# DeltaNet gate joined to the output projection, and layer-end steps shared out anew, in a two-layer hybrid backbone

## The chip, the core and the metric

The kernel runs on one core of a Trainium2 chip. The metric is the device time of one execution in microseconds (us). TensorE is PE, VectorE is DVE, ScalarE is ACT, GpSimd is POOL and SyncE is SP in the rows of the profile.

## The reference

Two post-norm layers act on 1024 latent tokens and 256 context tokens, with 1024 channels, all in float32. In each layer one input projection feeds four groups of heads (windowed attention, a gated DeltaNet, retention, latent attention), whose joined outputs go through one output projection, and then an MLP with squared ReLU follows. The parts that matter here are these:

```python
def layer_norm(x, g, b):
    mu = jnp.mean(xf, axis=-1, keepdims=True)
    var = jnp.mean(jnp.square(xf - mu), axis=-1, keepdims=True)
    return (xf - mu) * lax.rsqrt(var + LN_EPS) * g + b
...
    def out(o, z_):        # DeltaNet gate
        o = rms_norm(o.transpose(0, 2, 1, 3), norm_g) * silu(z_)
...
        y, yc = token_mixers(x * (1 + sc1) + sh1, xc * (1 + csc1) + csh1, ...)
        x = layer_norm(DEEPNORM_ALPHA * x + g1 * (y @ w_out[layer]), ln1_g[layer], ln1_b[layer])
        x = layer_norm(DEEPNORM_ALPHA * x + g2 * squared_relu_mlp(x * (1 + sc2) + sh2, ...),
                       ln2_g[layer], ln2_b[layer])
```

The context goes through the same steps in layer 0 only, and the output is the latent stream.

## The kernel before

**Layout.** Channels lie on the 128 partitions: `X[:, k, token]` holds block k of 8 channel blocks for 1280 tokens. Tokens are worked in segments, `SEGMENTS` = (0, 256), (256, 768), (768, 1280); the first is the context. Layer 1 needs no context output and uses the last two (`tokens(L)`), and its very end is cut as (256, 768), (768, 1024), (1024, 1280) (`end_tokens`).

**Products.** Each float32 operand of a large product is split into a high part (rounded to fp32r) and a low part (the rest), and a product is three matmuls per channel block: high by high, low by high, high by low. The high part of the projection's input is `H_hi`, a copy by ScalarE (L1773); the low part `Y_lo` is a subtraction on VectorE (L2459), written over `Y` itself. Weight halves come by DMA into a ring and are split in the same way, by ScalarE (`split_high`, L1466) and VectorE (`split_low`, L1986) outside the MLP, and by GpSimd (L2731, L2732) in it. `next_half` makes TensorE wait until a half is split (`w_split`).

**Order.** Every engine has an instruction list of its own, and semaphores tie them together. `nth` and `tally` keep the counts. `ln.barrier()` makes all four engines wait for one another, and `link` makes an engine wait for its own last result.

**The gate.** After the DeltaNet scan, and behind a barrier, `gate` runs on ScalarE and VectorE and `gate_turn` on TensorE, once in each layer. The scan's output `o` and the gate input `z` have tokens on the partitions, 10 tiles of 256 channels. ScalarE squares `o` (L1755), takes tanh(z/2) (L1756), splits the high part of a weight half, takes a root (L1760, with a table load ahead of it) and splits a second one. VectorE sums the squares per head (L2359), makes (tanh + 1) z (L2362), multiplies by the gain `dn_g` (L2364), splits a low part (L1986), inverts the root (L2368) and then, in five rounds of two tiles, scales and gates (L2372, L2374). Each round is transposed by TensorE (L762, four transposes) and copied from PSUM into `Y` by ScalarE (L1765). A second barrier follows, then `project_out`: high parts, low parts, and 24 matmuls (L751) for each of 8 output blocks and each segment. Sums for the next normalization are made on VectorE between them.

**The layer end.** After the last MLP group each segment goes through `layer_end`. Its column sum goes through a matmul with ones (`end_mean`, L1249), `centre` subtracts the mean (L2392, VectorE), `square` squares on ScalarE into `Hm` (L1787), `end_var` sums the squares with ones on TensorE (L1257), `root` (L1792) and `invert` (L2399) work in PSUM, `scale` multiplies (L2405), and `affine` applies gain and bias, eight ScalarE instructions per segment (L1874). At the end of layer 0 the next layer starts at once: `modulate_full` (L1995, VectorE) makes the modulated input, `modulate_high` (L1481, ScalarE) its high part, written over `X` once `X` has been saved to memory (`x_saved_*`, SP's queue), and `modulate_low` (L2005, VectorE) the low part. `mla_item` steps of the latent attention's preparation are woven in on all engines; their one-column steps on GpSimd are `mla_prep` (L2634). GpSimd has no other work at either layer end. At the end of layer 1 the output is sent by SP in six transfers, each behind an `ln_out` count.

GpSimd has a step of the same form as an affine step elsewhere, in the MLP's start: `TS(X, X, grown_g, grown_b)` at L2744.

## Time and profile before

| | |
|---|---|
| median of 3 runs | 4320.06 us (4316.73 to 4320.37) |
| profiled execution | 4329.14 us, its span 4327.3 us |
| mean granted TensorE clock | 0.955 |
| TensorE busy | 3989.3 us (92%) |
| VectorE busy | 2041.8 us (47%) |
| ScalarE busy | 1131.9 us (26%) |
| GpSimd busy | 937.3 us (22%) |

Busy time is a sum over the span; a span is the time from the first to the last instruction. In a timeline a row gives the start and the length in us, engine, line, operation, output and inputs, shapes, how many instructions were merged, and in brackets the idle time before it and what ended it. ACTq, DVEq and POOLq are the engines' sequencers. Layer 0 has its gate from 1209 us and its end from 2245 us; layer 1 has its gate from 3421 us and its end from 4270 us.

### The profile page before, as it was taken

The numbers are of one execution on the slowest core, as the hardware profiler recorded it, in microseconds if no ns is written. First come the engines' busy times: TensorE is split into PE (matmuls) and PEld (weight loads), VectorE is DVE, ScalarE is ACT, GpSimd is POOL, SyncE is SP. The second block draws the span as 40 slices with busy tenths as digits, with TensorE's granted clock in tenths as the row PEclk, the third lists the DMA queues.
The fourth block names the chain that finished last, engine by engine and source line by source line (L and its number), as shares of the span: only waits on it lengthen the run. The fifth ranks groups of instructions, "written<-read, shape, count | busy, mean of one in ns | idle before, by whom it ended". The sixth has DMA issues, their size and how long they took to land. (4 is left out here: it accounts for less than half of the span.)

```text
span 4327.3 us, 77639 instructions
## 1 busy us (share of the span) xinstructions
PE 3989.3 (92%) x33178; PEld 3278.3 (76%) x33178; DVE 2041.8 (47%) x3705; ACT 1131.9 (26%) x2456; POOL 937.3 (22%) x671
## 2 busy tenths in 40 slices
PE   6999988989979999999998999889899799999997
PEld 5655987778867888888886557778688677888886
DVE  3344546544456433333356344566344555443346
ACT  3344224233323111111115443232333311110012
POOL 0000110032202433333321000100223114444441
PEclk8898999999989999999998998999899899999999
DMA  4311000100010111111111110000100011111111
GB/s 168 117 79 59 21 30 1 76 3 3 3 49 10 39 39 39 39 39 39 39 38 69 59 79 30 20 21 20 48 3 3 21 39 39 49 48 48 48 49 49
DMA packets 27552, 181.00 MB, mean 42 GB/s; under 512 B 2560, under 2 KB 6912, under 8 KB 12032
## 3 DMA queue, kind: packets, MB, share of 16 engines
q1 hardware_dynamic: 25968, 173.69, 10.8%
q8 instruction: 226, 3.70, 0.4%
q10 hardware_dynamic: 1296, 3.10, 0.2%
q14 instruction: 62, 0.51, 0.0%
HBM read 168.39 MB, written 8.39 MB: 41 GB/s over the span
## 5 line engine op out<-in xcount | busy, mean ns | idle before, releaser
L1298 PE MATMUL ps<-Yn_parts,ring_parts 128*128 128x512 f32 (+1 forms) x3888 | 803.2, 368 | 11.5 <-issue 7.7
L1298 PEld LDWEIGHTS ps<-Yn_parts,ring_parts 128*128 128x128 f32 x3888 | 674.4, 190 | 137.3 <-issue 9.9
L1298 PE MATMUL ps<-temp_parts,ring_parts 128*128 128x512 f32 (+1 forms) x2560 | 727.9, 370 | 3.9 <-DVE Hn_parts L2437 3.9
L2731 POOL TENSOR_TENSOR ring_parts<-ring,consts 128x2048 fp32r<-128x2048 f32 x64 | 295.6, 4619 | 1209.1 <-DMA ring<-in_ff 1093.6
L741 PE MATMUL ps<-ring_parts,Xn_parts 128*128 128x256 f32 x2560 | 514.6, 296 | 28.3 <-DVE ring_parts L1986 12.8
L2384 DVE SCALAR_TENSOR_TENSOR Xn<-ps,mods,Xn 128x256 f32<-128x256 f32 (+1 forms) x364 | 251.8, 692 | 604.0 <-PE ps L1298 503.3
L1298 PEld LDWEIGHTS ps<-temp_parts,ring_parts 128*128 128x128 f32 x2560 | 466.4, 190 | 88.3 <-DVE Hn_parts L2437 5.9
L1298 PE MATMUL ps<-Hn_parts,ring_parts 128*128 128x512 f32 (+1 forms) x1280 | 472.1, 369 | 0.0
L741 PEld LDWEIGHTS ps<-ring_parts,Xn_parts 128*128 128x128 f32 x2560 | 425.8, 199 | 32.3 <-issue 23.5
L1825 ACT ACTIVATE Yn<-ps 128x256 f32<-128x256 f32 (+1 forms) x160 | 88.7, 554 | 1265.7 <-PE ps L1298 1265.7
L2491 DVE TENSOR_TENSOR Yn<-Yn 128x256 f32<-128x256 f32 (+1 forms) x160 | 200.6, 1254 | 406.2 <-ACT Yn_parts L1827 406.2
L741 PE MATMUL ps<-ring_parts,Hn_parts 128*128 128x256 f32 x1280 | 371.7, 290 | 0.0
L762 PE MATMUL ps<-consts,temp 128*128 128x128 f32 (+1 forms) x1416 | 259.3, 300 | 94.4 <-DVE temp L2087 23.6
L762 PEld LDWEIGHTS ps<-consts,temp 128*128 128x128 f32 (+1 forms) x1416 | 175.9, 149 | 212.0 <-issue 96.4
L2732 POOL TENSOR_TENSOR ring_parts<-ring,ring_parts 128x2048 fp32r<-128x2048 f32 x64 | 302.2, 4722 | 5.0
L1298 PEld LDWEIGHTS ps<-Hn_parts,ring_parts 128*128 128x128 f32 x1280 | 242.4, 189 | 40.5
L741 PEld LDWEIGHTS ps<-ring_parts,Hn_parts 128*128 128x128 f32 x1280 | 255.8, 200 | 1.2 <-issue 0.2
L862 PE MATMUL ps<-Yn,temp 96*128 96x512 f32 (+1 forms) x400 | 199.0, 612 | 8.0 <-ACT temp L1565 3.9
L2339 DVE TENSOR_TENSOR ring<-ps,Hn 128x256 f32<-128x256 f32 x200 | 84.7, 423 | 237.3 <-PE ps L1168 236.3
L2492 DVE TENSOR_TENSOR Yn_parts<-Yn,Yn_parts 128x256 fp32r<-128x256 f32 (+1 forms) x160 | 193.0, 1206 | 5.5
L1730 ACT ACTIVATE ring<-ps 128x256 f32<-128x256 f32 x240 | 91.6, 382 | 363.3 <-PE ps L1179 310.2
L1576 ACT ACTIVATE temp<-ps 128x512 f32<-128x512 f32 (+1 forms) x200 | 103.8, 520 | 231.1 <-PE ps L762 217.9
(310 smaller groups left out, 5956.0 us busy)
## 6 DMA issues: line engine op xcount, KB each, us to landing
ring<-in_ff SPq DMA_DIRECT2D x64, 1024.0 KB, 4.7
ring<-in_ada SPq DMA_DIRECT2D x22, 2048.0 KB, 8.9
ring<-in_halves SPq DMA_DIRECT2D x28, 1024.0 KB, 4.8
Xn<-in_x SPq DMA_DIRECT2D x2, 5120.0 KB, 25.0
Hn<-in_ada SPq DMA_DIRECT2D x2, 2048.0 KB, 20.9
kept_x<-Xn SPq DMA_DIRECT2D x4, 1024.0 KB, 4.0
Xn<-kept_x SPq DMA_DIRECT2D x1, 4096.0 KB, 14.9
Hn<-in_halves SPq DMA_DIRECT2D x2, 1024.0 KB, 7.6
```

The source lines that it names most:

```text
L741: m = pe.matmul(ps[:, bank, 0:256], (G_hi, H_lo)[a][:, k, t * P:(t + 1) * P], w[b][:, k, :], start=(k == 0 and part == 0), stop=(k == KT - ...
L762: return pe.transpose(out, src, ident[0:rows, 0:rows])
L862: m = pe.matmul(m_flat[:, base + a:base + b], m_q[0:96, h, t * P:(t + 1) * P], m_k[0:96, h, a:b], start=True, stop=True, skip_group_check= ...
L1298: m = pe.matmul(ps[:, bank, 0:hi - lo], w[a][:, k, j * P:(j + 1) * P], x[b][:, k, lo:hi], start=(k == 0 and part == 0), stop=(k == k_n - 1 ...
L1576: A(m_pT[:, k0:k1, :], ps[:, 5 + c % 2, 0:(k1 - k0) * P].rearrange("p (a b) -> p a b", b=P), ACT.Copy)\
L1730: A(flat(b["lower"]), ps[:, q, 0:256], ACT.Copy).then_inc(sems[f"u_lower{q}"], tally(f"u_lower{q}"))
L1825: ln.link(A(U[:, j, lo:hi], ps[:, n_ % 4, 0:hi - lo], ACT.Relu))
L2384: return STT(X[:, j, lo:hi], ps[:, bank, 0:hi - lo], mods[:, L, gate_ + j, which:which + 1], X[:, j, lo:hi], ALU.mult, ALU.add)
L2491: link(TT(u_, u_, u_, ALU.mult))
L2492: TT(U_lo[:, j, lo:hi], u_, U_hi[:, j, lo:hi].bitcast(F32), ALU.subtract).then_inc(sems["hidden"], tally("hidden"))
L2731: link(TT(by(half_hi[s]), by(half[s]), spread(ones, 1, HALF // P), ALU.mult))
L2732: TT(half_lo[s], half[s], half_hi[s].bitcast(F32), ALU.subtract).then_inc(sems["split"], tally("split"))
```

## The change

The gate of both layers: the squares and their sums are made in two halves. The gain is no longer a multiplication on VectorE but the scale of the copies out of PSUM, where channels lie on partitions (`dn_g` becomes one column of the parameters). VectorE's low split moves behind the five rounds. The barrier ahead of `project_out` goes. ScalarE makes the first segment's high parts between its third and fourth copy, upper channel blocks first, and TensorE's first product, `first_product`, takes all matmuls on high parts before those on low parts. `out_free` is raised behind the last copy.

The layer ends: `affine` and, for the last two segments at the end of layer 0, `modulate_high` are halved, channel blocks 0 to 3 on ScalarE and 4 to 7 on GpSimd, with waits that keep the counts in order. At the end of layer 0 the square sum of segment 1 goes ahead of the mean of segment 2 on TensorE, and the centring of segment 2 moves behind the scaling of segment 1 on VectorE. At the end of layer 1 the centring of the last segment moves ahead of the scaling of the first.

```diff
+            def first_product(w, lo, hi):
+                halves_ = (range(4, KT), range(4))
+                for n_, ks in enumerate(halves_):
+                    pe.wait_ge(sems["h_high"], nth("h_high", n_ + 1))
+                    for k in ks:
+                        for a in range(2):
+                            pe.matmul(ps[:, 0, 0:hi - lo], w[a][:, k, 0:P], H_hi[:, k, lo:hi], start=(k == 4 and a == 0), stop=False)
+                pe.wait_ge(sems["h_split"], nth("h_split", 1))
+                for ks in halves_:
+                    for k in ks:
+                        m = pe.matmul(ps[:, 0, 0:hi - lo], w[0][:, k, 0:P], Y_lo[:, k, lo:hi], start=False, stop=(k == 3))
                 m.then_inc(sems["prod"], tally("prod"))
...
+                    if n_ == 0:
+                        first_product(halves_[i], *cols[c])
+                        continue
...
                 if L + 1 < DEPTH:
+                    end_var(L, 1)
                     end_mean(L, 2)
-                    end_var(L, 1)
                     mla_item(L + 1, 0)
+                    mla_item(L + 1, 1)
                     end_var(L, 2)
-                    for i in range(1, 2 * NT + 3):
+                    for i in range(2, 2 * NT + 3):
...
                 gate_turn(gate_dn)
-                ln.barrier()
...
-                for k in range(KT):
-                    if L and c and k % 4 == 0:
-                        act.wait_ge(sems[f"x_saved_{2 * (c - 1) + k // 4}"], 16)
+                for k in range(4 if L and c else KT):
+                    if L and c and k == 0:
+                        act.wait_ge(sems[f"x_saved_{2 * (c - 1)}"], 16)
+                    if L and c == 2 and k == 3:
+                        act.wait_ge(sems["h_high"], nth("h_high", 4 * len(tokens(L - 1)) + 2 * c))
...
-            def gate(g_):
-                A(g_["sq"].rearrange("p a b -> p (a b)"), g_["o"], ACT.Square).then_inc(sems["sq_done"], tally("sq_done"))
+            def gate(g_, L):
+                lo, hi = tokens(L)[0]
+                sq = flat(g_["sq"])
+                for c in range(2):
+                    n_ = NT * 128
+                    A(sq[:, c * n_:(c + 1) * n_], g_["o"][:, c * n_:(c + 1) * n_], ACT.Square).then_inc(sems["sq_done"], tally("sq_done"))
                 A(flat(g_["th"]), flat(g_["z"]), ACT.Tanh, scale=0.5).then_inc(sems["g_tanh"], tally("g_tanh"))
-                if g_ is gate_dn:
-                    split_high()
+                split_high()
                 act.wait_ge(sems["g_veps"], nth("g_veps", 1))
                 A(g_["root"], g_["root"], ACT.Sqrt).then_inc(sems["g_rstd"], tally("g_rstd"))
-                if g_ is gate_dn:
-                    split_high()
+                split_high()
                 for c in range(NT // 2):
+                    if c == 3:
+                        act.wait_ge(sems["g_y"], nth("g_y", NT // 2))
+                        for n_ in range(3):
+                            act.wait_ge(sems["yT_sb"], nth("yT_sb", n_ + 1))
+                        for k in (4, 0):
+                            A(H_hi[:, k:k + 4, lo:hi], Y[:, k:k + 4, lo:hi], ACT.Copy).then_inc(sems["h_high"], tally("h_high"))
                     act.wait_ge(sems["yT_mm"], nth("yT_mm", c + 1))
-                    A(Y[:, g_["rows"]:g_["rows"] + 2, 2 * c * P:2 * (c + 1) * P], ps[:, 5 + c % 2, :].rearrange("p (a b) -> p a b", a=2), ACT.Copy)\
-                        .then_inc(sems["yT_sb"], tally("yT_sb"))
+                    A(Y[:, g_["rows"]:g_["rows"] + 2, 2 * c * P:2 * (c + 1) * P], ps[:, 5 + c % 2, :].rearrange("p (a b) -> p a b", a=2), ACT.Copy,
+                      scale=g_["gain"]).then_inc(sems["yT_sb"], tally("yT_sb"))
             def project_out(L):
                 cols = tokens(L)
+                act.wait_ge(sems["yT_sb"], nth("yT_sb", NT // 2))
                 act.sem_inc(sems["out_free"], 1)
...
                     for k in (0, 4):
-                        A(H_hi[:, k:k + 4, lo:hi], Y[:, k:k + 4, lo:hi], ACT.Copy).then_inc(sems["h_high"], tally("h_high"))
+                        if c:
+                            A(H_hi[:, k:k + 4, lo:hi], Y[:, k:k + 4, lo:hi], ACT.Copy).then_inc(sems["h_high"], tally("h_high"))
...
                 def affine(c):
                     lo, hi = cols[c]
-                    for b in range(2):
-                        act.wait_ge(sems["ln_scaled"], nth("ln_scaled", 2 * c + b + 1))
-                        for k in range(4 * b, 4 * b + 4):
-                            m = A(X[:, k, lo:hi], X[:, k, lo:hi], ACT.Identity, bias=ln2_b[:, k:k + 1], scale=ln2_g[:, k:k + 1])
-                        m.then_inc(sems["ln_out"], 1)
+                    act.wait_ge(sems["ln_scaled"], nth("ln_scaled", 2 * c + 1))
+                    for k in range(4):
+                        if k == 3 and c:
+                            act.wait_ge(sems["ln_out"], 2 * len(SEGMENTS) * L + 2 * c)
+                        m = A(X[:, k, lo:hi], X[:, k, lo:hi], ACT.Identity, bias=ln2_b[:, k:k + 1], scale=ln2_g[:, k:k + 1])
+                    m.then_inc(sems["ln_out"], 1)
...
                 root(0)
                 square(1)
                 affine(0)
+                root(1)
                 modulate_high(L + 1, 0)
-                root(1)
-                square(2)
+                affine(1)
                 act.wait_ge(sems["params_in"], 16)
                 mla_item(0)
-                affine(1)
-                root(2)
+                square(2)
                 mla_item(1)
                 modulate_high(L + 1, 1)
+                root(2)
                 mla_item(2)
                 affine(2)
                 mla_item(3)
...
             def gate(g_):
                 heads, th = (lambda ap, n: ap.rearrange("p (h c) -> p h c", h=n)), flat(g_["th"])
-                n_gain = g_["gain"].shape[1]
-                dve.wait_ge(sems["sq_done"], nth("sq_done", 1))
-                link(dve.tensor_reduce(g_["root"], g_["sq"], AX.X, ALU.add))
+                for c in range(2):
+                    n_ = NT * H // 2
+                    dve.wait_ge(sems["sq_done"], nth("sq_done", c + 1))
+                    m = dve.tensor_reduce(g_["root"][:, c * n_:(c + 1) * n_], g_["sq"][:, c * n_:(c + 1) * n_, :], AX.X, ALU.add)
+                link(m)
                 TS(g_["root"], g_["root"], 1.0 / 64, EPS, ALU.mult, ALU.add).then_inc(sems["g_veps"], tally("g_veps"))
                 dve.wait_ge(sems["g_tanh"], nth("g_tanh", 1))
-                link(STT(th, th, 1.0, flat(g_["z"]), ALU.add, ALU.mult))
-                th_ = heads(th, NT * 256 // n_gain)
-                link(TT(th_, th_, spread(g_["gain"], 1, NT * 256 // n_gain), ALU.mult))
-                if g_ is gate_dn:
-                    split_low()
+                STT(th, th, 1.0, flat(g_["z"]), ALU.add, ALU.mult)
                 dve.wait_ge(sems["g_rstd"], nth("g_rstd", 1))
                 link(dve.reciprocal(g_["rs"], g_["root"]))
                 for c in range(NT // 2):
...
                     for a in range(2):
                         m = STT(pairs(g_["out"], c)[:, a], o_[:, a], 0.5, pairs(g_["th"], c)[:, a], ALU.mult, ALU.mult)
                     m.then_inc(sems["g_y"], tally("g_y"))
+                split_low()
+                ln.passed("sq_done", 2)
...
                 for c, (lo, hi) in enumerate(cols):
-                    for b in range(2):
+                    for n_, b in enumerate((0, 1) if c else (1, 0)):
                         ks = slice(4 * b, 4 * b + 4)
-                        dve.wait_ge(sems["h_high"], nth("h_high", 2 * c + b + 1))
+                        dve.wait_ge(sems["h_high"], nth("h_high", 2 * c + n_ + 1))
...
                 if L + 1 == DEPTH:
+                    centre(2)
                     scale(0)
-                    centre(2)
                     invert(1)
                     scale(1)
                     invert(2)
                     scale(2)
                     return
                 modulate_full(L + 1, 0)
+                invert(1)
+                modulate_low(0)
+                scale(1)
                 centre(2)
-                modulate_low(0)
-                invert(1)
-                scale(1)
                 mla_item(0)
                 modulate_full(L + 1, 1)
-                invert(2)
                 mla_item(1)
                 modulate_low(1)
+                invert(2)
                 scale(2)
                 mla_item(2)
                 modulate_full(L + 1, 2)
...
+            def affine(L, c):
+                lo, hi = end_tokens(L)[c]
+                pool.wait_ge(sems["ln_scaled"], nth("ln_scaled", 2 * len(tokens(L)) + 2 * c + 2))
+                for k in range(4, KT):
+                    if k == KT - 1:
+                        pool.wait_ge(sems["ln_out"], 2 * len(SEGMENTS) * L + 2 * c + 1)
+                    m = TS(X[:, k, lo:hi], X[:, k, lo:hi], ln2_g[:, k:k + 1], ln2_b[:, k:k + 1], ALU.mult, ALU.add)
+                m.then_inc(sems["ln_out"], 1)
+            def modulate_high(L, c):
+                mod, (lo, hi) = mods[:, L], SEGMENTS[c]
+                which = 1 if lo < NCTX else 0
+                pool.wait_ge(sems["h_seg"], nth("h_seg", c + 1))
+                pool.wait_ge(sems[f"x_saved_{2 * (c - 1) + 1}"], 16)
+                for k in range(4, KT):
+                    if k == KT - 1:
+                        pool.wait_ge(sems["h_high"], nth("h_high", 4 * len(tokens(L - 1)) + 2 * c + 1))
+                    m = TS(G_hi[:, k, lo:hi], X[:, k, lo:hi], mod[:, SC1 + k, which:which + 1], mod[:, SH1 + k, which:which + 1], ALU.mult, ALU.add)
+                m.then_inc(sems["h_high"], tally("h_high"))
+            def layer_end(L):
+                affine(L, 0)
+                affine(L, 1)
+                if L + 1 == DEPTH:
+                    affine(L, 2)
+                    return
+                mla_prep(0, 2)
+                modulate_high(L + 1, 1)
+                mla_prep(2, 3)
+                affine(L, 2)
+                mla_prep(3, 4)
+                modulate_high(L + 1, 2)
+                mla_prep(4, 2 * NT)
+            def mla_prep(first=0, end=2 * NT):
```

## Rows read from the trace of the kernel before

**Rows 1.** Waits of the whole span, TensorE: waiter, releaser, us, times, longest

```profile
PE ps L762 <- DVE Hn L2374: 37.0, 10, 17.5
...
PE ps L751 <- DVE Yn_parts L2459: 12.0, 2, 7.5
```

**Rows 2.** Timeline, ScalarE, gate of layer 0: start us, us, instruction, idle before

```profile
1209.17 2.34 ACT L1755 ACTIVATE Hn<-temp 128x2560 f32<-128x2560 f32 x1 [8.36 <-POOLq L211]
1211.41 2.32 ACT L1756 ACTIVATE Hn<-temp 128x2560 f32<-128x2560 f32 x1
...
1215.74 1.28 ACT L1760 ACT_TABLE_LOAD   x1
1217.04 0.24 ACT L1760 ACTIVATE Hn<-Hn 128x40 f32<-128x40 f32 x1
...
1231.98 9.20 ACT L1773 ACTIVATE temp_parts<-Yn 128x1024 fp32r<-128x1024 f32 x6 [0.20 <-ACTq L211]
```

**Rows 3.** Timeline, VectorE, gate of layer 0

```profile
1211.60 2.82 DVE L2359 TENSOR_REDUCE Hn<-Hn 128x40 f32<-128x2560 f32 x1 [2.71 <-ACT Hn L1755]
...
1214.55 2.82 DVE L2362 SCALAR_TENSOR_TENSOR Hn<-Hn,temp 128x2560 f32<-128x2560 f32 x1
1217.40 2.82 DVE L2364 TENSOR_TENSOR Hn<-Hn,params 128x2560 f32<-128x2560 f32 x1
1220.26 2.29 DVE L1986 TENSOR_TENSOR ring_parts<-ring,ring_parts 128x2048 fp32r<-128x2048 f32 x1
...
1222.90 0.69 DVE L2372 TENSOR_TENSOR temp<-temp,Hn 128x512 f32<-128x512 f32 x1
...
1229.21 0.76 DVE L2374 SCALAR_TENSOR_TENSOR Hn<-temp,Hn 128x256 f32<-128x256 f32 x2
```

**Rows 4.** Timeline, TensorE, around both gates

```profile
1224.53 1.09 PE L762 MATMUL ps<-consts,Hn 128*128 128x128 f32 x4 [17.44 <-DVE Hn L2374]
...
1235.65 0.77 PE L751 MATMUL ps<-temp_parts,ring_parts 128*128 128x256 f32 x2 [4.50 <-DVE Yn_parts L2459]
...
3450.49 1.19 PE L751 MATMUL ps<-temp_parts,ring_parts 128*128 128x512 f32 x2 [7.49 <-DVE Yn_parts L2459]
```

**Rows 5.** Timeline, ScalarE, gate of layer 1

```profile
3421.02 2.34 ACT L1755 ACTIVATE Hn<-temp 128x2560 f32<-128x2560 f32 x1 [8.37 <-POOLq L211]
...
3426.43 1.91 ACT L1466 ACTIVATE ring_parts<-ring 128x2048 fp32r<-128x2048 f32 x1 [0.85 <-DMA ring<-in_halves]
```

**Rows 6.** Windows, TensorE: length, busy (instructions), granted clock, DMA share, GB/s

```profile
1228.00:1231.20 3.20, 2.58 (x10) 0.50 0.00 0
1238.00:1240.60 2.60, 2.60 (x14) 0.50 0.02 6
```

**Rows 7.** Timeline, VectorE, end of layer 0

```profile
2292.17 4.49 DVE L2405 TENSOR_TENSOR Xn<-Xn,ps 128x2048 f32<-128x2048 f32 x2
...
2310.54 4.48 DVE L2405 TENSOR_TENSOR Xn<-Xn,ps 128x2048 f32<-128x2048 f32 x2
...
2322.87 1.92 DVE L1995 TENSOR_SCALAR Hn<-Xn,mods 128x512 f32<-128x512 f32 x4 [0.91 <-ACT Xn L1874]
...
2331.66 2.29 DVE L2005 TENSOR_TENSOR Hn_parts<-Hn,Xn_parts 128x2048 fp32r<-128x2048 f32 x1 [0.53 <-ACT Xn_parts L1481]
```

**Rows 8.** Timeline, ScalarE, end of layer 0: affine steps of segment 1

```profile
2294.49 5.75 ACT L1874 ACTIVATE Xn<-Xn,small 128x512 f32<-128x512 f32 x8 [1.77 <-DVE Xn L2405]
```

**Rows 9.** Timeline, TensorE, end of layer 0: its longest idle time

```profile
2310.73 0.55 PE L741 MATMUL ps<-ring_parts,Xn_parts 128*128 128x256 f32 x1 [9.82 <-issue]
```

**Rows 10.** Instructions of line 2744 (GpSimd): duration ns min/median/max

```profile
L2744 POOL TENSOR_SCALAR Xn<-Xn,small x40: 548/778/1720, 1383.5 to 3602.0; 128x512 f32<-128x512 f32 x32, 128x256 f32<-128x256 f32 x8
```

**Rows 11.** Timeline near the end of layer 1: a GpSimd split, a VectorE step

```profile
4220.85 4.62 POOL L2731 TENSOR_TENSOR ring_parts<-ring,consts 128x2048 fp32r<-128x2048 f32 x1 [13.49 <-DMA ring<-in_ff]
4221.22 4.79 DVE L2491 TENSOR_TENSOR Yn<-Yn 128x512 f32<-128x512 f32 x1 [3.94 <-ACT Yn_parts L1827]
```

**Rows 12.** Timeline, ScalarE, end of layer 1: the last affine steps

```profile
4320.09 4.04 ACT L1874 ACTIVATE Xn<-Xn,small 128x256 f32<-128x256 f32 x8 [3.09 <-DVE Xn L2405]
```

More of the change, by code:

```diff
@@ L753, in channel_product @@
                 m.then_inc(sems["prod"], tally("prod"))
+            def first_product(w, lo, hi):
[9 more added lines that the diff above has]
+                        m = pe.matmul(ps[:, 0, 0:hi - lo], w[0][:, k, 0:P], Y_lo[:, k, lo:hi], start=False, stop=(k == 3))
+                m.then_inc(sems["prod"], tally("prod"))
             def arrived(j=0):
@@ L1940, in _ @@
                 act.sem_inc(sems["half_free"], 2)
-                gate(gate_dn)
-                ln.barrier()
+                gate(gate_dn, L)
                 project_out(L)
@@ L2628, in _ @@
             TT, TS, COPY = pool.tensor_tensor, pool.tensor_scalar, pool.tensor_copy
-            def mla_prep():
-                for u in range(2 * NT):
+            def affine(L, c):
[30 more added lines that the diff above has]
+            def mla_prep(first=0, end=2 * NT):
+                for u in range(first, end):
                     w_ = 256 if u < NT else 128
@@ L2772, in _ @@
                 ln.barrier()
-                ln.barrier()
                 mlp(L)
-                if L + 1 < DEPTH:
-                    mla_prep()
+                layer_end(L)
             ln.barrier()
@@ L2837, in pack_params @@
         "log1m_row": np.repeat(g, 32, axis=1).T, "a_log": rows(w["dn_a_log"][L]), "dt": rows(w["dn_dt_bias"][L]),
-        "dn_g": rows(w["dn_norm_g"][L]), "ret_g": rows(w["ret_norm_g"][L]), "ln1_g": chan(w["ln1_g"][L]),
+        "dn_g": np.tile(w["dn_norm_g"][L], 2)[:, None], "ret_g": rows(w["ret_norm_g"][L]), "ln1_g": chan(w["ln1_g"][L]),
         "ln1_b": chan(w["ln1_b"][L]), "ln2_g": chan(w["ln2_g"][L]), "ln2_b": chan(w["ln2_b"][L]), "conv": conv,
```

3 lines of the change are left out of this document (1 added, 2 removed).

## The prediction

> **What bounds the kernel now.** I began with the profile's table of engines: TensorE is busy 92% of the span, so the other engines can give back only time in which TensorE stands still or runs at its low clock. The waits of TensorE come next, longest in total first. The reader is to see that the longest one is for the gate of the DeltaNet heads, and that the low parts of the projection's input are another [rows 1]. The timelines then show how each wait comes about.
>
> At the gate, ScalarE makes the squares and the tanh, then loads a table and takes the root [rows 2]. VectorE adds up the squares, makes silu of z (2.82 us), multiplies by the gain (2.82 us) and splits a weight half (2.29 us), all before its first normalization step, which starts 13.7 us after the first square [rows 3]. TensorE meanwhile idles 17.4 us; after the last transpose it idles again, 4.5 us in layer 0 and 7.5 us in layer 1, until the first segment has both its parts [rows 4]. Once the projection runs, TensorE's waits are short, so I take a start that is earlier by some time to be worth that time.
>
> At the end of layer 0 VectorE is the full engine: centring, scaling, modulation and low parts follow one another in its queue [rows 7], ScalarE's eight affine steps per segment pace the modulation [rows 8], and TensorE's longest idle time there is 9.8 us [rows 9]. At the end of layer 1 nothing follows but the output's transfer, and the last affine steps are on the path [rows 12].
>
> **The gate, layer 0.** I count from the first square's start, T = 1209.17. With the squares in halves, a half costs about 1.2 us (half of 2.34), and a half of the sum about 1.5 (half of 2.82 and a fixed part) [rows 2, 3]. The second half of the sum ends near T+4.3 instead of T+5.3. The tanh ends near T+4.7, so silu runs T+4.8 to T+7.6. ScalarE splits one weight half, then loads its table and takes the root, as before; the root was ready at T+8.1 [rows 2] and is now at T+8.2. The gain multiplication leaves the queue (it rides on the copies out of PSUM, whose number is the same), and the low split moves behind the loop. So reciprocal and first step start at T+8.7, where it was T+13.7: 5.0 us sooner. The loop's five rounds end 7.1 us after its start [rows 3], at T+15.8. Then comes the low split, until T+18.0. This split used to be covered by nothing and isn't now either: `next_half` makes TensorE wait for it. It is the last thing before the product, because the first high part (1024 columns, about 0.9 us, at the pace of the six copies, 10,240 columns in 9.2 us [rows 2]) starts at T+15.9 and is ready at T+16.9, and the last transposes end at T+17.1. TensorE starts at T+18.1, where it was 1235.65, T+26.5 [rows 4]: 8.4 us.
>
> `first_product` has eight matmuls on each half of the high parts before it needs low parts, 3.4 us at the low clock (0.21 us each for 256 columns). The low parts come at T+20.4, so no stall appears there; at the full clock one of 0.6 us would. Behind it ScalarE still owes two copies out of PSUM and the second segment's high parts, and VectorE the low parts, near T+25.5; TensorE needs them at T+26. That cover is thin: a microsecond late is a microsecond lost.
>
> **The gate, layer 1.** T is 3421.02. Here the weight half arrives late and ScalarE's split starts at T+5.4 [rows 5], so the root is ready only at T+8.9, which is now what VectorE waits for. First step at T+9.4 (from T+13.7), loop end at T+16.5, split until T+18.8. The high part is 512 columns wide (1.9 us) and is ready at T+18.5. TensorE started at 3450.49, T+29.5 [rows 4], and now starts at T+18.8: 10.7 us. More than half of this comes from behind the loop: both high parts (3.8 us) and low parts stood ahead of the product.
>
> **TensorE's clock at the gates.** The granted clock was 0.50 (1.2 GHz) both during the transposes and from 2.4 to 5 us into the projection [rows 6]. The idle time ahead of the transposes shrinks from 17 to 12 us, and the gap behind them from 4.5 to 1.1 us. I take the same stretch at the low clock as before. The bound on the other side is a clock that rises at once: some 5 us at half speed cost 2.5 us per layer, so 5 us in all.
>
> **The end of layer 0.** I ran the VectorE queue forward in its new order. The variance of segment 1 goes ahead of the mean of segment 2, while TensorE was waiting for that mean's sum, so the root is there about 9 us earlier. Scaling of segment 1 ends near 2290.8 instead of 2296.7 [rows 7], but the centring of segment 2 (as large, an estimate of 4.5 us) now stands behind it. GpSimd's four affine steps, at 0.78 us for 512 columns [rows 10], are done at 2294, where ScalarE's eight ended at 2300.2 [rows 8]. Modulation and low parts of segment 1 end 2.6 us sooner, at 2308.0 instead of 2310.6; the inversion (3.4 us) that used to fill the wait now follows, so scaling of segment 2 ends at 2315.8, 0.8 us later than before [rows 7]. With halves of affine and high part on GpSimd, the last modulation ends near 2322.5 (2324.8 before) and the last low part near 2332.3 (2333.95 before) [rows 7]: 1.7 us. TensorE's transposes behind them wait for VectorE's next step.
>
> From that comes off what the port costs. A VectorE step with two SBUF inputs that is 0.69 us elsewhere took 4.79 us while GpSimd was in a 4.62 us instruction, and ended 0.5 us after it [rows 11, 3]. GpSimd's first four affine steps now run while VectorE adds up the last sums, which costs about 0.7 us. I keep 1.0 us of gain. The same thing in the skill's words: the page "SBUF — State Buffer", section "Who interferes with whom", says that the second read and write port is an exclusive lock between VectorE and GpSimd, held for a whole instruction, that a VectorE instruction with two SBUF inputs or in a two-port mode takes part in it, and one with a PSUM input doesn't. The trace agrees as far as its 4.79 us goes. That rule speaks against giving GpSimd work beside modulation and low parts; the rival below puts a price on it from rows.
>
> Bounds for this stage: GpSimd's step ranges from 0.55 to 1.72 us in the trace [rows 10]. Were every one 1.72 us, four would take 6.9 instead of 3.1; that happens up to four times on the path, of which VectorE has other work beside two, so 8 us of loss. On the other side, if the port costs nothing and TensorE enters segment 1 warm after its idle time [rows 9], 4 us of gain.
>
> **The end of layer 1.** Centring of segment 2 ahead of the scaling of segment 0 costs: the scaling starts some 3.8 us later (2.4 for a centring of 256 columns, 1.4 for its mean). ScalarE's affine steps for segment 0 halve from 5.75 (the width of [rows 8]) to 2.9, so its next root is about 1 us late. The affine steps of segment 1 halve from 4.0 to 2.0 and turn that into 1 us early. The last steps took 4.04 us on ScalarE [rows 12]; GpSimd starts its four when the second half is scaled, 1.2 us later, and needs 4 times about 0.6: 3.6 in all, 0.4 sooner. I take 1.3 us; bounds -1 and +2.5.
>
> **Sum.** 8.4 + 10.7 + 1.0 + 1.3 = 21.4 us. The profiled execution took 4329.1 us with a span of 4327.3; the same would be 4307.7 with a span near 4306. It lies 9 us above the median of the runs, so I subtract from the median: 4320.1 - 21.4 = 4298.7.
>
> **Rivals.** (a) The clock rises as soon as the projection starts, since the gap ahead of it is now 1 us. For it: the shorter gap. Against it: transposes that kept TensorE busy 2.58 of 3.20 us left the clock at 0.50 [rows 6]. It gives 21.4 + 5 = 26, so 4294. (b) GpSimd's share at the layer ends blocks VectorE, by the lock described above. For it: rows 11. Against it: the steps are 0.78 us long, not 4.6, and VectorE's centring, scaling and inversion read PSUM. Its price is 9 us against my 1.0, so 4307. (c) The thin cover behind the first product fails: the low parts of segment 1 and the evacuations come late, as VectorE starts the projection with its queue full. It would return up to 12 of the 19 us, so 4311, which is hardly told from no change. (d) Slower: the alternating waits between ScalarE and GpSimd at the end of layer 0 make each segment wait for GpSimd. Its sixteen 512-column steps there would all have to be on the path, and cost more than 21.4 + 8.6 us together, 1.9 us above the 0.78 each; from 2.7 us a step on it decides, and the time there is 4329. The longest step in the trace is 1.72 [rows 10].
>
> **Chances.** The forecast 0.70, (a) 0.10, (b) 0.12, (c) 0.05, (d) 0.03. The forecast's own range is 4293 to 4304. To leave out no more than 2 in 10 it goes down to 4290 (some of the clock) and up to 4309 (the port's price). A measurement of this kernel can't tell less than 0.2% (8.6 us) from no change, which is 4311.4. Faster by more: 0.90, since only (d) and most of (c) and a little of (b) lie above; within: 0.07; slower: 0.03.
>
> **What would show it.** In the profile after, the first transpose of each gate starts some 5 and 4.3 us sooner after the squares, and the projection's first matmul at T+18.1 and T+18.8, released by the split on VectorE. The chain there holds no 2.82 us gain step. At the end of layer 0 the last low part lies only 1 to 2 us nearer to the last product than before. The prediction is wrong if TensorE shows new waits of over 2 us within the projection, if GpSimd's affine steps take over 1.5 us, or if VectorE's modulation and low parts at the layer end grow by over 5 us in sum.

## The result and the profile after

The changed kernel takes 4292.47 us (median of 4 runs, 4291.69 to 4294.81), the kernel before beside it 4320.22 (4 runs, 4316.73 to 4329.01). The ratio is 0.9931, with a 95% interval of 0.9917 to 0.9946: faster by 27.7 us, where I forecast 21.4. A later job with the same kernel gave 4288.00 (6 runs, 4282.70 to 4291.33) beside 4315.59, ratio 0.9927 (0.9906 to 0.9948).

The first view of the kernel after is TensorE's waits: waiter, releaser, us, times, longest. They answer to [rows 1].

```profile
PE ps L776 <- DVE Hn L2402: 26.9, 10, 12.4
...
PE ps L762 <- DVE ring_parts L2016: 2.2, 2, 1.1
```

The wait for the gate went from 37.0 to 26.9 us, and the two waits for low parts, 12.0 together, are gone. In their place stand two waits for the split of a weight half, 2.2 us. The timeline of the gate of layer 0 shows how. VectorE, kernel after (start, length, instruction, idle before):

```profile
1211.53 2.88 DVE L2390 TENSOR_REDUCE Hn<-Hn 128x20 f32<-128x1280 f32 x2 [1.65 <-ACT Hn L1779]
1214.44 0.18 DVE L2392 TENSOR_SCALAR Hn<-Hn 128x40 f32<-128x40 f32 x1
1214.85 2.83 DVE L2394 SCALAR_TENSOR_TENSOR Hn<-Hn,temp 128x2560 f32<-128x2560 f32 x1 [0.22 <-ACT Hn L1780]
1218.44 0.40 DVE L2396 RECIPROCAL Hn<-Hn 128x40 f32<-128x40 f32 x1 [0.76 <-ACT Hn L1783]
1218.88 0.69 DVE L2400 TENSOR_TENSOR temp<-temp,Hn 128x512 f32<-128x512 f32 x1
...
1225.86 2.29 DVE L2016 TENSOR_TENSOR ring_parts<-ring,ring_parts 128x2048 fp32r<-128x2048 f32 x1
```

ScalarE and then TensorE, same kernel and stretch, TensorE also at the gate of layer 1:

```profile
1210.16 2.43 ACT L1779 ACTIVATE Hn<-temp 128x1280 f32<-128x1280 f32 x2 [8.36 <-DVEq L211]
...
1218.17 0.24 ACT L1783 ACTIVATE Hn<-Hn 128x40 f32<-128x40 f32 x1
...
1225.98 2.00 ACT L1791 ACTIVATE temp_parts<-Yn 128x1024 fp32r<-128x1024 f32 x2 [0.93 <-DVE Hn L2402]
1227.89 1.25 ACT L1793 ACTIVATE Yn<-ps,params 128x512 f32<-128x512 f32 x2
```

```profile
1220.51 1.09 PE L776 MATMUL ps<-consts,Hn 128*128 128x128 f32 x4 [12.42 <-DVE Hn L2402]
...
1228.20 3.78 PE L762 MATMUL ps<-temp_parts,ring_parts 128*128 128x256 f32 x16 [1.08 <-DVE ring_parts L2016]
...
3415.81 5.78 PE L762 MATMUL ps<-temp_parts,ring_parts 128*128 128x512 f32 x16 [1.08 <-DVE ring_parts L2016]
```

With T = 1210.16 the loop starts at T+8.7, the split ends at T+18.0 and the product starts at T+18.0, released by the split. That is the forecast's course to a tenth of a microsecond. Against [rows 4] the idle time ahead of the transposes fell from 17.4 to 12.4 us, and the gap behind them from 4.5 to 1.1 (from 7.5 to 1.1 in layer 1).

To see where the rest comes from I cut each profiled execution at the same seven instructions: the start of the first square of each gate (T0, T1) and of the first matmul of each projection (P0, P1), and the end of the last column sum of layer 0 (S), of the last low part of the modulation behind it (Q) and of the last column sum of layer 1 (E). The kernels of the other rows are those of the experiments below; after_again is the kernel after in the later job. Stages in us:

```
                 start-T0  T0-P0    P0-S    S-Q     Q-T1   T1-P1   P1-E   E-end   span
before            1209.17  26.48  1042.31  55.99  1087.07  29.47  848.86  27.95  4327.3
after             1210.16  18.04  1041.36  52.86  1075.46  17.93  847.87  26.22  4289.9
after_again       1207.02  17.88  1041.40  52.85  1075.68  17.88  846.88  26.21  4285.8
gate_only         1206.56  17.88  1041.13  55.72  1076.52  18.50  846.35  27.94  4290.6
gate_late         1208.85  21.96  1040.65  55.81  1076.76  25.31  845.99  27.97  4303.3
gate_split_first  1209.78  18.37  1043.70  56.05  1086.87  19.22  847.05  27.96  4309.0
gain_back         1208.56  20.17  1042.39  52.94  1076.18  20.17  845.94  26.65  4293.0
ends_only         1201.87  26.48  1042.91  52.93  1075.89  29.46  847.00  27.46  4304.0
ends_order        1209.67  26.48  1042.54  53.12  1076.01  29.48  848.86  31.44  4317.6
ends_share        1205.62  26.49  1042.60  58.78  1076.83  29.47  846.83  24.08  4310.7
after_old_end     1209.10  17.91  1041.50  52.84  1075.69  18.04  847.56  23.26  4285.9
filled            1209.37  17.93  1042.29  54.01  1087.30  18.13  844.73  23.24  4297.0
```

From before to after the four changed stages give 8.44 + 3.13 + 11.54 + 1.73 = 24.84 us. The stretches behind the products give 0.95 and 0.99, the start takes back 0.99 (it scatters from 1201.9 to 1210.2 whatever the kernel), and Q to T1, the latent attention of layer 1, which no edit touches, gives 11.61. The spans differ by the sum, 37.4.

That last stage has two levels over these executions, 1075.5 to 1076.8 or 1086.9 to 1087.3. TensorE's clock goes with them. Here is one of several stretches in which it differs, about 271 us behind Q in both: a window of the kernel before, then of the kernel after (length, busy and instructions, granted clock, DMA share, GB/s):

```profile
2605.00:2620.00 15.00, 14.65 (x65) 0.66 0.37 141
```

```profile
2593.00:2608.00 15.00, 12.98 (x91) 1.00 0.38 141
```

The kernel before stands at a lower clock and gets through 65 instructions where the other does 91. The level looks like one of the execution, not of the kernel. Among the profiles it was long with the old gate (before) and with the new one (gate_split_first, filled), with the old layer ends (before, gate_split_first) and with the new ones (filled), and it was short with either gate (ends_only, gate_only) and either layer ends (gate_only, after). Of the 66 runs of the kernel before in all jobs, 43 took 4304.2 to 4320.9 us and 23 took 4325.6 to 4335.1, with nothing between, and the profiled one (4329.1) is of the second group. The profiled execution of gate_split_first (4310.8) has the long stage too, and is the only one of its 6 runs above 4298.6. So 11.6 of the 37.4 us are, as far as this shows, no work of the change; no kernel was profiled at both levels. The medians are less exposed: in the later job the lower group's median is 4313.7 (8 of the 11 runs), and the kernel after is 25.7 us below it.

### The profile page after: what moved, and what is told of

The parts are those of the page before. It is cut to its first block, busy times and chain, and to the rows that moved or that the text cites. A ratio compares the mean times of both kernels' runs of the same rounds, so it can differ in the third digit from the quotient of the medians.

```text
span 4289.9 us, 77635 instructions
## 1 busy us (share of the span) xinstructions
PE 3974.2 (93%) x33178; PEld 3269.9 (76%) x33178; DVE 2032.5 (47%) x3705; ACT 1114.4 (26%) x2426; POOL 967.7 (23%) x703
## 4 chain that ended last, share of the span: by engine, by line
PE 83%; DVE 10%; ACT 3%; issue 2%; POOL 1%; DMA 1%; DVEq 0%; POOLq 0%; SPq 0%; ACTq 0%
PE ps L1315 36%; PE ps L741 9%; PE ps L751 7%; PE ps L776 4%; PE ps L876 4%; PE ps L1182 3%; PE ps L915 3%; PE ps L1190 2%; PE ps L1193 2%; PE ps L785 1%; PE ps L1271 1%; PE ps L1148 1%; PE ps L979 1%; PE ps L1245 1%; PE ps L1232 1%
## 5 line engine op out<-in xcount | busy, mean ns | idle before, releaser
L2521 DVE TENSOR_TENSOR Yn<-Yn 128x256 f32<-128x256 f32 (+1 forms) x160 | 177.9, 1112 | 406.8 <-ACT Yn_parts L1857 406.8
L2522 DVE TENSOR_TENSOR Yn_parts<-Yn,Yn_parts 128x256 fp32r<-128x256 f32 (+1 forms) x160 | 210.0, 1312 | 5.5
## 6 DMA issues: line engine op xcount, KB each, us to landing
Xn<-kept_x SPq DMA_DIRECT2D x1, 4096.0 KB, 15.8
```

The source lines that it names most:

```text
L2521: link(TT(u_, u_, u_, ALU.mult))
L2522: TT(U_lo[:, j, lo:hi], u_, U_hi[:, j, lo:hi].bitcast(F32), ALU.subtract).then_inc(sems["hidden"], tally("hidden"))
```

## The experiments

**The two halves of the change.** gate_only has the gate's edits and the old layer ends, ends_only the layer ends and the old gate.

> The gate's edits of both layers without those of the layer ends. Theory A (the parts are independent and add up): the traces show the gate of layer 0 worth 9.5 us and that of layer 1 worth 12.9, so this kernel is 22 us faster than before (20 to 24), near 4298; the projection starts 18.0 us after the first square in both layers, and the stage between the end of layer 0 and the gate of layer 1 takes as long as in the kernel before. Theory B (part of the 27.7 us is TensorE's clock in the latent attention of layer 1, which shifts with any shift ahead of it): 11 us of the difference between the two profiles lie in that attention; then this kernel gains up to 10 us more or less than 22, and the difference sits between the end of layer 0 and the gate of layer 1.

> The edits of the two layer ends without those of the gate. Theory A: 3.4 us at the end of layer 0 and 1.8 at the end of layer 1, so 5 us faster than before (3 to 7), near 4315; the traces put the last low part of the modulation 3 us nearer to the last sum. Theory of the prediction (GpSimd's port eats most of it): 2.3 us faster. Theory B (clock in the attention behind it): anything from 6 us slower to 15 faster, with the difference in the latent attention of layer 1.

Measured: gate_only 4296.52 us (9 runs: eight of 4292.40 to 4306.33, and one of 9642.72), ratio 0.9945 (0.9926 to 0.9964). ends_only 4313.88 (12 runs), ratio 0.9983 (0.9969 to 0.9997), both against 4319.22 (32 runs, nearly half of them in the upper group). The 17 runs of the lower group have a median of 4313.66: gate_only is 17.1 us below it, ends_only is no different from it. So the gate carries the gain, and that of the layer ends shows in the stages alone. The gate's stages shrink by 8.6 and 11.0 us; the layer ends by 3.1 and 0.5. The end of layer 1 is 0.5 here and 1.7 in the kernel after with the same edits there: TensorE's last 16 square sums took 6.63 us at a granted clock of 0.55 here, 5.15 at 0.71 there.

**What the early start is worth.** gate_late keeps the halved squares, the gain on the copies and the split behind the loop, but has the barrier back, all high parts behind it, and the old order of the first product (the cut is against gate_only).

```diff
                 gate_turn(gate_dn)
+                ln.barrier()
                 project_out(L)
...
                 for n_, (i, c, j) in enumerate(out_order(L)):
-                    if n_ == 0:
-                        first_product(halves_[i], *cols[c])
-                        continue
```

> As the gate's edits alone, but the barrier ahead of the projection is back, the first segment's high parts stand behind all copies, and the first product has its usual order; the gain on the copies, the squares in halves and the split behind the loop stay. Theory A (starting the high parts early and not waiting for low parts is worth more than half): TensorE starts the projection about 22.3 us after the first square in layer 0 and 25.2 in layer 1, so this kernel loses 4.2 + 7.3 = 11.5 us against the gate's edits alone and is some 10 us faster than before. Rival (the gain's 2.8 us and the split are the whole story, the rest is hidden): it loses under 3 us against the gate's edits alone.

Measured: 4305.17 us (10 runs), ratio 0.9963 (0.9947 to 0.9980), 8.7 us above gate_only, where I expected 11.5. The waits before the first product, TensorE and ScalarE of gate_late:

```profile
1230.81 0.77 PE L751 MATMUL ps<-temp_parts,ring_parts 128*128 128x256 f32 x2 [4.87 <-DVE Yn_parts L2476]
```

```profile
1227.14 5.60 ACT L1791 ACTIVATE temp_parts<-Yn 128x1024 fp32r<-128x1024 f32 x4 [0.47 <-DVEq L211]
```

The high parts start at T+18.3 instead of T+15.8 and the product waits 4.87 us for low parts, as in [rows 4]. By stages the early start is worth 4.1 and 6.8 us, 10.9 in sum; the medians of two kernels differ from their stages by 2 us easily, with runs spread over 9 to 14. The forecast's split of the gate into a part ahead of the loop and a part behind it holds.

**The gain multiplication.** gain_back is the kernel after with the gain on VectorE again.

```diff
-                STT(th, th, 1.0, flat(g_["z"]), ALU.add, ALU.mult)
+                link(STT(th, th, 1.0, flat(g_["z"]), ALU.add, ALU.mult))
+                th_ = heads(th, NT * 4)
+                link(TT(th_, th_, spread(g_["gain"], 1, NT * 4), ALU.mult))
```

> The kernel after with the gain multiplication back on VectorE as one instruction of 2.82 us ahead of the reciprocal, and the copies out of PSUM without a gain. In the kernel after VectorE waits 0.76 us for the root there, so the loop should start 2.82 - 0.76 = 2.06 us later in layer 0, and in layer 1 too, a little less where the root comes later. The copies cost 0.6 instead of 0.69 us, which lies beside VectorE's steps. The first projection matmul should come at 20.1 us after the first square in layer 0 and at 19.9 in layer 1. Time 4 us above the kernel after. The rival: ScalarE's first high part and the copies, not VectorE, set the product's start, and the shift is smaller.

Measured: 4293.92 us (6 runs) beside 4288.00 for the kernel after, 5.9 more. VectorE in gain_back, with T = 1208.56:

```profile
1216.11 2.82 DVE L2395 TENSOR_TENSOR Hn<-Hn,params 128x2560 f32<-128x2560 f32 x1
1218.97 0.40 DVE L2397 RECIPROCAL Hn<-Hn 128x40 f32<-128x40 f32 x1
1219.41 0.69 DVE L2401 TENSOR_TENSOR temp<-temp,Hn 128x512 f32<-128x512 f32 x1
```

The loop starts at T+10.85 instead of T+8.72, and the products at T+20.17 in both layers, 2.1 to 2.3 us later: the 2.82 less the wait of 0.76 for the root that it fills. The rival, that ScalarE sets the start, falls.

**The low split.** gate_split_first is gate_only with `split_low()` in front of the reciprocal, where VectorE waits for the root.

> The gate's edits alone, with the low split of the weight half ahead of the loop again. Prediction's theory (the split is the last thing ahead of the product wherever it stands; ahead of the loop it fills VectorE's wait for the root): the loop starts 1.5 us later, the split is gone behind it, and the projection starts 18.6 us after the first square in layer 0 (17.9 with the split behind) and 19.2 in layer 1 (18.5): 1 to 2 us slower than the gate's edits alone. Rival (each microsecond on VectorE counts the same): no difference.

Measured: 4297.31 us (6 runs), ratio 0.9958 (0.9943 to 0.9974); not to be told from gate_only, by medians of two jobs. The products start at T+18.37 and T+19.22, against 17.88 and 18.50, as the forecast's theory had it. The loop starts at T+10.07 instead of T+8.72, 1.35 us later: the split's 2.29 less the wait that it fills. Behind the loop no split follows, and the product starts right behind the last transpose. So the split costs 1.35 us ahead of the loop and about 1 behind it, where the transposes would end anyway; its place matters little.

**The clock.** filled is after_old_end (below) with matmuls on constants ahead of and between the transposes, whose results nobody reads.

```diff
             def gate_turn(g_):

+                fill(13, 512)
                 for c in range(NT // 2):
+                    if c:
+                        fill(1, 256)
```

> As the one before, with matmuls on constants that nothing reads in TensorE's idle time at both gates (13 of 512 columns ahead of the transposes, one of 256 between them). Theory A (the rest of TensorE's low clock at the gates costs little, since the low parts from VectorE bound the first segment): the clock is 1.00 when the projection starts, layer 1 gains 1.5 us from there to the end and layer 0 gains 0 to 0.5, as TensorE waits for the second segment's low parts instead. Theory of the clock (what the chip lost there is half of 4 us per layer): 2 us in each. The start itself, 18.0 us after the first square, doesn't move, unless the added matmuls delay a transpose.

Measured: 4289.98 us (6 runs, 4279.85 to 4298.82), ratio 0.9934 (0.9916 to 0.9953), not to be told from after_old_end's 4286.98 with a spread of 19 us. First the clock of the kernel after at the product of layer 0, then of filled, then TensorE in filled:

```profile
1228.20:1230.00 1.80, 1.80 (x8) 0.50 0.00 0
1230.00:1232.00 2.00, 2.00 (x12) 0.53 0.00 0
1232.00:1234.00 2.00, 2.00 (x19) 1.00 0.03 8
```

```profile
1228.00:1230.00 2.00, 1.89 (x16) 1.00 0.00 0
```

```profile
1227.30 2.16 PE L762 MATMUL ps<-temp_parts,ring_parts 128*128 128x256 f32 x16 [0.52 <-DVE ring_parts L2025]
...
1235.22 0.72 PE L751 MATMUL ps<-temp_parts,ring_parts 128*128 128x512 f32 x2 [1.55 <-DVE Yn_parts L2498]
```

At the full clock the first 16 matmuls take 2.16 instead of 3.78 us, and TensorE then stands still for 1.55 us until VectorE has the next segment's low parts. In layer 0 the microseconds of the clock are owed to VectorE; this is the thin cover of the forecast, come true where TensorE is faster. P0 to S is 0.8 and S to Q 1.2 us longer than in after_old_end; in layer 1 P1 to E is 2.8 us shorter, which the medians don't show. (The long Q to T1 of this execution is the level told of above.)

**Order or share at the layer ends.** ends_order has the new orders of TensorE, ScalarE and VectorE alone; ends_share has GpSimd's halves alone, in the old orders, both with the old gate. The core of the one and of the other:

```diff
                 if L + 1 < DEPTH:
+                    end_var(L, 1)
                     end_mean(L, 2)
-                    end_var(L, 1)
                     mla_item(L + 1, 0)
```

```diff
                 mlp(L)
-                if L + 1 < DEPTH:
-                    mla_prep()
+                layer_end(L)
```

> Only the new orders at the layer ends (square sum ahead of the mean, centring moved, roots and squares moved on ScalarE); all affine steps and high parts stay on ScalarE. Theory A1 (the order alone gives the gain at the end of layer 0, GpSimd's share adds nothing there since it waits for the saved X or holds the port): 3.5 us sooner at the end of layer 0 and 1 us later at the end of layer 1, in all 2.5 us faster. Theory A2 (the share is what gives it): about 0.5 us sooner at the end of layer 0, 1 us later at the end of layer 1, in all no gain.

> Only the halves on GpSimd (affine steps and high parts) and none of the new orders; the gate is that of before. If the order gave the whole gain at the end of layer 0 (2.9 us with the order alone, 3.1 with both), the halves alone give under 1 us there, since GpSimd waits for the saved X and for VectorE. If both are ways to the same gain, they give 2 to 3 us there too. At the end of layer 1 the old order with halves takes 23 us from the last sum to the end (28.0 before, 27.5 with both edits, 31.4 with the order alone): the centring ahead of the scaling costs 4 us, and the halves are worth 5. In all 6 to 8 us faster than before; if the centring costs nothing, 1 to 2.

Measured: ends_order 4317.82 us (10 runs), ratio 0.9994 (0.9977 to 1.0010); ends_share 4316.65 (10 runs), ratio 1.0001 (0.9989 to 1.0013). Neither differs from before in time; against the lower groups of their jobs (4313.66 and 4313.05) they are even 4 us slower, of which the stages show 0.6 us at most; the rest stays open. The stages do differ. At the end of layer 0 the order alone gives 2.9 us and the halves alone cost 2.8. At the end of layer 1 it is the other way round: the order costs 3.5, the halves give 3.9. GpSimd, then VectorE, of ends_share at the end of layer 0:

```profile
2293.36 3.04 POOL L2640 TENSOR_SCALAR Xn<-Xn,small 128x512 f32<-128x512 f32 x4 [19.44 <-DVE Xn L2408]
2296.48 0.19 POOL L2674 TENSOR_SCALAR small<-small 128x1 f32<-128x1 f32 x1
2296.76 0.56 POOL L2675 TENSOR_TENSOR small<-small 128x1 f32<-128x1 f32 x1
```

```profile
2297.36 0.48 DVE L2047 TENSOR_SCALAR temp<-ps,small 128x256 f32<-128x256 f32 x1 [4.10 <-POOL small L2675]
```

The affine steps are quick. The loss begins where the small steps of the next layer's first item, which VectorE waits for, now stand behind them in GpSimd's queue: VectorE waits 4.10 us, where the kernel before didn't wait at all. Counted from S, the modulation of segment 1 then ends 2.6 us later than before, and the scaling of segment 2 still does. The halves win back 1.4 us of it by the next low part, and lose it again at the last one, for which VectorE waits 2.19 us for GpSimd's high part (0.53 for ScalarE's before).

**The centring at the end of layer 1.** after_old_end puts the scaling of segment 0 ahead of the centring of segment 2 again.

```diff
                 if L + 1 == DEPTH:
-                    centre(2)
                     scale(0)
+                    centre(2)
                     invert(1)
```

> The changed kernel, with the scaling of the first segment ahead of the centring of the last again at the end of layer 1. If that centring is on the path, the end takes 23 us from the last sum, 3.3 less than in the changed kernel, and the kernel takes 4289. If not, 4292 as the changed kernel.

> The kernel after, unchanged, as the yardstick for the two kernels beside it on the same chip. Its gates should start the first projection matmul 18.04 and 17.93 us after the first square again. Open is the clock of layer 1's latent attention: if its two levels belong to an execution and not to a kernel, this profile of the same kernel may show the stage (last modulation's low part at the end of layer 0 to the first square of layer 1's gate) at either about 1075.5 or about 1087 us; if the level belonged to the kernel, it has to be 1075.5 again, as in the first profile of this kernel. Median about 27 us below the kernel before, ratio 0.9937.

> The kernel after with the scaling of segment 0 ahead of the centring of segment 2 at the end of layer 1, now beside the kernel after on one chip. From the profiled stages (26.22 us from the last column sum to the end in the kernel after, 23.26 in this one) it should be 3 us faster than the kernel after by medians. The rival is that the 5.5 us between their earlier medians was real: then the order also gives something outside that stage.

Measured: after_old_end 4286.98 us (6 runs), ratio 0.9934 (0.9917 to 0.9950); then on one chip the kernel after 4288.00 (6 runs) and after_old_end, as old_end_again, 4288.95 (6 runs, 4282.98 to 4290.31), ratio 0.9928 (0.9907 to 0.9949). The last stage is 2.97 us shorter in both profiles (23.26 and 23.24 against 26.21). VectorE of the kernel after:

```profile
4264.99 2.36 DVE L2422 SCALAR_TENSOR_TENSOR Xn<-ps,Xn 128x1024 f32<-128x1024 f32 x2 [1.31 <-PE ps L1263]
4267.27 4.47 DVE L2435 TENSOR_TENSOR Xn<-Xn,ps 128x2048 f32<-128x2048 f32 x2
4274.76 1.77 DVE L2429 RECIPROCAL ps<-ps 128x256 f32<-128x256 f32 x1 [3.01 <-ACT ps L1822]
```

and of after_old_end:

```profile
4262.56 4.48 DVE L2435 TENSOR_TENSOR Xn<-Xn,ps 128x2048 f32<-128x2048 f32 x2
4266.96 2.35 DVE L2422 SCALAR_TENSOR_TENSOR Xn<-ps,Xn 128x1024 f32<-128x1024 f32 x2
4270.77 1.77 DVE L2429 RECIPROCAL ps<-ps 128x256 f32<-128x256 f32 x1 [1.46 <-ACT ps L1822]
```

The centring waits 1.31 us for its sum and takes 2.36, while the scaling could run. The medians of six runs, spread over 7 to 9 us, can't show 3 us: the old order is the better one by the stage, and not shown better in time. So no version is shown to beat the kernel after.

## Why the prediction was right, step by step

**Gate, layer 0 (8.4 us): right.** First loop step at T+8.72 (forecast 8.7), first product at T+18.04 (18.1), 8.4 us. gate_late and gain_back show its two larger terms one at a time.

**Gate, layer 1 (10.7 us): right in mechanism, 0.8 short.** It gave 11.5. The product starts at T+17.93, not T+18.8. I had carried over the 0.85 us wait of [rows 5] for the weight half; in the kernel after ScalarE's split starts without a wait, in gate_only with one of 0.58 us, and its product at T+18.50. Why the half comes in time in the one and not in the other isn't shown.

**The stall behind the first product: right.** Nothing over 1.1 us shows in the two projections. Rival (c) lives in filled alone, with a stall of 1.55 us.

**The clock: between forecast and rival (a).** I kept the low stretch as it was, at 5 us. By windows of 0.5 us from the product's start on, the granted clock was 0.50 for 5.4 us in the kernel before and 3.7 in the kernel after in layer 0, and for 5.8 and 4.0 us in layer 1. The 1.7 and 1.8 us less at half speed are worth 0.9 us each, 1.8 in both, against nothing in the forecast and 5 in the rival. P0 to S and P1 to E are 0.95 and 0.99 us shorter, which fits, but both scatter by 3 us over the executions without fillers, so they can't carry it alone (gate_split_first took 1043.70 from P0 to S with 3.5 us of low clock, gate_late 1040.65 with 3.4). That the shorter gap did it isn't shown, and two rows speak against it: gain_back, behind the same gap of 1.1 us, stayed at 0.50 for 5.2 us, and gate_late, behind one of 4.9, for only 3.4.

**End of layer 0 (1.0 us): the term that was mis-sized; it measured 3.1.** My forward run of the queue was good up to the last items. Shifted by the 8.4 us of the gate, scaling of segment 1 ends at 2290.8 (forecast the same), modulation and low parts at 2307.6 (2308.0), the last modulation at 2321.8 (2322.5). The last low part ends at 2330.8, not 2332.3: 3.1 us sooner instead of 1.7. And the 0.7 us that I took off for the port was 0.24 (0.93 us instead of 0.69), which falls ahead of S and so isn't in the 3.1; with it the gain is 2.9 against my 1.0. VectorE and GpSimd of the kernel after:

```profile
2266.86 0.93 DVE L2443 TENSOR_TENSOR temp<-temp,Xn 128x512 f32<-128x512 f32 x1
2267.97 0.75 DVE L2414 SCALAR_TENSOR_TENSOR Xn<-ps,mods,Xn 128x512 f32<-128x512 f32 x1 [0.18 <-DVE temp L2443]
...
2287.16 3.73 DVE L2025 TENSOR_SCALAR Hn<-Xn,mods 128x512 f32<-128x512 f32 x8
...
2308.78 4.57 DVE L2025 TENSOR_SCALAR Hn<-Xn,mods 128x512 f32<-128x512 f32 x8
...
2320.13 2.29 DVE L2035 TENSOR_TENSOR Hn_parts<-Hn,Xn_parts 128x2048 fp32r<-128x2048 f32 x1 [1.43 <-POOL Xn_parts L2678]
```

```profile
2291.06 2.28 POOL L2678 TENSOR_SCALAR Xn_parts<-Xn,mods 128x512 fp32r<-128x512 f32 x3 [0.59 <-DVEq L2027]
2294.01 2.87 POOL L2678 TENSOR_SCALAR Xn_parts<-Xn,mods 128x512 fp32r<-128x512 f32 x1 [0.67 <-ACT Xn_parts L1500]
...
2307.11 3.23 POOL L2666 TENSOR_SCALAR Xn<-Xn,small 128x512 f32<-128x512 f32 x4 [1.36 <-DVE Xn L2435]
...
2314.89 5.21 POOL L2678 TENSOR_SCALAR Xn_parts<-Xn,mods 128x512 fp32r<-128x512 f32 x4 [3.32 <-DMA kept_x<-Xn]
2320.18 2.29 POOL L2700 TENSOR_SCALAR small<-small 128x1 f32<-128x1 f32 x1
```

Most of the port's price falls on GpSimd, not on VectorE, which is the full engine: a GpSimd step of 0.77 us takes 2.87 beside a 2.29 us low part, and one of 0.19 us on a single column takes 2.29. VectorE pays where it waits for those steps (0.68 and 1.43 us here, 0.52 and 0.53 for ScalarE's in ends_order), and in one place that I had not priced: the modulation of segment 2, which has only one tensor input, takes 4.57 us beside GpSimd's affine steps instead of 3.73. In sum that is 1.9 us in VectorE's queue behind S, where rival (b) wanted 8 us more on the path. It leaves the share almost nothing at this end: 3.1 us with it, 2.9 without.

What I had not seen is that the share needs the order. The gain there is that of the new orders (ends_order); GpSimd's halves cost 2.8 us unless the orders are moved, because of the small steps in its queue. Had only the share been made, my cost of the steps themselves would have given the wrong sign.

**End of layer 1 (1.3 us): right, 1.7.** Its terms were 3.8 us of loss by the centring and 5.1 of gain by the halves, of which after_old_end against the kernel after and before shows 3.0 and 4.7.

**Rival (d): excluded.** GpSimd's four affine steps take 3.0 to 3.2 us at 512 columns and 2.2 to 2.6 at 256, the longest step 0.99; only a step beside a VectorE low part passed 1.7. The last ones of the kernel after, which answer to [rows 12]:

```profile
4271.85 3.03 POOL L2666 TENSOR_SCALAR Xn<-Xn,small 128x512 f32<-128x512 f32 x4 [57.51 <-DVE Xn L2435]
...
4284.50 2.17 POOL L2666 TENSOR_SCALAR Xn<-Xn,small 128x256 f32<-128x256 f32 x4 [3.32 <-DVE Xn L2435]
```

**The sum.** The four stages give 24.8 us where I forecast 21.4, and the clock 1.8, 26.6 together. The 25.7 against the lower group and the 27.7 of the medians lie within 1.1 us of that on either side, which is less than the runs scatter. The time, 4292.5, lies in the range, and just below the 4293 of the forecast's own. That it lies inside is in part luck: the forecast started from a median of 4320.1, and in the later job, with 4315.59 before, the same kernel took 4288.00, below the range's 4290, at the same ratio.

## What to carry to other kernels

Cost a gate or another joint by running each engine's queue forward from one common event, and name the last releaser: three steps of this forecast held to 0.1 us that way. When work moves to an engine with idle time, cost what is queued behind it there, small steps that others wait for above all; here, in ends_share, that outweighed what the share gave. And cut two profiles into stages at the same instructions before explaining the difference of their spans: 11.6 of 37.4 us came from a stage that nobody touched.

## What the runs showed of the hardware

The latent attention of layer 1 ran in 1075.5 to 1076.8 or in 1086.9 to 1087.3 us, at a granted clock of 1.00 or 0.66 in 15 us at the same place of it, with neither the gate nor the layer ends going with it; the kernel before fell into its upper group of times in 23 of 66 runs, the kernel after in none of 10. What decides is open, and I didn't find which activity ahead of the stage goes with either.

A GpSimd instruction that starts beside a VectorE low part (two SBUF inputs, 2.29 us) ends behind it: 0.19 us became 2.29 and ended 0.05 us after it, 0.77 became 2.87 and ended 0.65 us after it. The reverse, 0.69 us of VectorE that became 4.79 beside a 4.62 us GpSimd instruction [rows 11], stood ahead of the prediction, and at the layer ends it was 0.93 at most, since the GpSimd steps there are short. A VectorE step with one tensor input in SBUF paid as well: two of the modulation's, 0.54 us alone, took 0.92 and 0.99 beside GpSimd's affine steps. The Trainium skill's page "SBUF — State Buffer", section "Who interferes with whom", has it as an exclusive lock held for a whole instruction; both directions agree.

ScalarE's copy of 512 columns out of PSUM takes 0.69 us with a gain for each partition and 0.60 without (gain_back), which nothing waits for here.
